# A latent-attention kernel: the next head group's projections one step sooner, and the second query tile's spread sums behind the next group's transposes

## The reference

```
q  = rms_norm(q_lat)  @ w_q_up    # 16 heads of 64 + 32
kv = rms_norm(kv_lat) @ w_kv_up   # 16 heads of 64 + 64
q_nope, q_pe = rms_norm(q[..., :64]), rope(rms_norm(q[..., 64:]))
k_nope, v    = rms_norm(kv[..., :64]), kv[..., 64:]
s = (q_nope . k_nope + q_pe . k_pe) * 96 ** -0.5
p = softmax(s);  o = p @ v;  o = o @ w_out
```

## Time and profile before

| | |
|---|---|
| median of 3 runs | 1421.31 us (1418.82 to 1421.77) |
| the profiled execution | 1419.54 us, of which 1417.7 us is the span of the trace |
| head of group 0 to the end of group 3 in the trace | about 1041.6 to 1195.2 us |
| PE busy (share of the span) | 1327.6 us (94%) |
| DVE, ACT busy | 838.3 us (59%), 553.0 us (39%) |
| instructions | 16585 |

### The profile page before, as it was taken

One profiled execution on the slowest core, in us unless ns is written; L12 is line 12 of the kernel. 1 busy time (PEld: TensorE's weight loads), 2 busy tenths in 40 slices (PEclk: granted clock), 3 DMA queues, 4 the chain that ended last, 5 costly groups with the idle time before them and its releaser, 6 DMA issues.

```text
span 1417.7 us, 16585 instructions
## 1 busy us (share of the span) xinstructions
PE 1327.6 (94%) x6816; PEld 1065.0 (75%) x6816; DVE 838.3 (59%) x1170; ACT 553.0 (39%) x737; POOL 6.5 (0%) x20
## 2 busy tenths in 40 slices
PE   6999879999899999999999999999978878799998
PEld 5877658888777787867777777787866556688887
DVE  5665666668664455662525262527766676667777
ACT  5354354454421222422222222224545555554542
POOL 0000000000000000000000000000000000000000
PEclk9999989999999999999999999999989999899999
DMA  8436375544645532264545444322211130445541
GB/s 325 181 119 252 119 282 186 190 159 180 235 149 208 208 119 90 97 245 163 196 160 190 166 177 180 119 82 70 83 64 36 73 120 13 166 141 205 187 178 60
DMA packets 23926, 218.79 MB, mean 154 GB/s; under 512 B 3120, under 2 KB 8240, under 8 KB 10672
## 3 DMA queue, kind: packets, MB, share of 16 engines
q1 hardware_dynamic: 21472, 209.67, 40.1%
q10 hardware_dynamic: 1520, 4.98, 0.9%
q0 software_dynamic: 864, 3.15, 0.6%
HBM read 216.74 MB, written 1.05 MB: 154 GB/s over the span
## 4 chain that ended last, share of the span: by engine, by line
PE 73%; DVE 14%; ACT 6%; issue 4%; DMA 2%; SPq 0%; DVEq 0%; ACTq 0%
PE bank L503 18%; PE bank L505 17%; PE bank L504 17%; PE bank L515 7%; DVE w_lo L1569 5%; PE bank L516 4%; ACT w_hi L1069 3%; PE mod_ps L552 3%; PE turned L531 2%; PE bank L920 2%; DVE scaled L1610 2%; DVE gated L1924 1%; PE small L928 1%; DMA raw<-in_w_branch 1%; DVE h L1831 1%
## 5 line engine op out<-in xcount | busy, mean ns | idle before, releaser
L1569 DVE TENSOR_TENSOR w_lo<-raw,w_hi 128x2048 fp32r<-128x2048 f32 (+4 forms) x168 | 338.0, 2053 | 84.8 <-ACT w_hi L1069 84.8
L1069 ACT ACTIVATE w_hi<-raw 128x2048 fp32r<-128x2048 f32 (+4 forms) x168 | 280.1, 1715 | 206.5 <-PE bank L505 169.0
L503 PE MATMUL bank<-act_parts,w_hi 128*128 128x512 f32 (+1 forms) x600 | 225.1, 375 | 1.8 <-DVE act_parts L1594 1.8
L515 PE MATMUL bank<-act_parts,w_hi 128*128 128x512 f32 x608 | 216.6, 400 | 6.7 <-DVE act_parts L1594 4.2
L504 PE MATMUL bank<-act_parts,w_hi 128*128 128x512 f32 (+1 forms) x600 | 221.8, 370 | 0.0
L505 PE MATMUL bank<-act_parts,w_lo 128*128 128x512 f32 (+1 forms) x600 | 221.6, 369 | 0.0
L516 PE MATMUL bank<-act_parts,w_lo 128*128 128x256 f32 x608 | 171.4, 282 | 0.0
L503 PE MATMUL bank<-w_hi,h_hi 128*128 128x512 f32 x392 | 155.3, 396 | 7.0 <-DVE h_lo L1846 3.6
L504 PE MATMUL bank<-w_lo,h_hi 128*128 128x512 f32 x392 | 153.4, 391 | 0.0
L505 PE MATMUL bank<-w_hi,h_lo 128*128 128x512 f32 x392 | 153.2, 391 | 0.0
L515 PEld LDWEIGHTS bank<-act_parts,w_hi 128*128 128x128 f32 x608 | 115.5, 190 | 35.1 <-DVE act_parts L1594 4.6
(11 more groups left out here) (262 smaller groups left out, 1650.2 us busy)
## 6 DMA issues: line engine op xcount, KB each, us to landing
raw<-in_ffn SPq DMA_DIRECT2D x35, 2048.0 KB, 7.9
raw<-in_mlp SPq DMA_DIRECT2D x24, 2048.0 KB, 7.8
raw<-in_mod_gate SPq DMA_DIRECT2D x7, 2048.0 KB, 8.0
raw<-in_conv_in SPq DMA_DIRECT2D x8, 1536.0 KB, 7.3
raw<-in_w_gates SPq DMA_DIRECT2D x4, 2048.0 KB, 8.2
raw<-in_w_branch SPq DMA_DIRECT2D x4, 2048.0 KB, 7.9
raw<-in_mla_q SPq DMA_DIRECT2D x4, 1152.0 KB, 5.2
raw<-in_w_out SPq DMA_DIRECT2D x2, 2048.0 KB, 8.3
```

The costliest lines, as they stand in the source:

```text
L503: te.matmul(dst, sh, mh, start=(j == 0), stop=False)
L515: te.matmul(b[:, :].rearrange("p (a t) -> p a t", a=2), sh, act_parts[:, :, 0, j, :], start=(j == 0), stop=False)
L1069: act.activation(w_hi[:, s, part], raw[:, at % 2, part], ACT.Copy).then_inc(hi_ready, 1)
L1569: ve.tensor_tensor(w_lo[:, s, part], raw[:, at % 2, part], w_hi[:, s, part].bitcast(f32), ALU.subtract).then_inc(lo_ready, 1)
```

## The change

Three things are moved; nothing is added or taken away.

1. PE does `project(1)` straight behind `project(0)` in step 0, and each later one a step sooner: steps 0 to 4 hold j = (0, 1), 2, 3, 4, 5, and steps 5 to 7 none.
2. ACT takes (0), (1), (2, 3), (4), (5) in steps 0 to 4, with its squares and its weight split tied to the same `take` as before. DVE's five pieces (`query_sums`, `query_gains`, the split, `query_rotation`, `key_sums`) each go one step up.
3. For groups 0 to 2, `spread_sums` of the second query tile leaves the end of its group and stands in the next group's head, behind the transposes of keys and queries and ahead of the scores.

```diff
--- before.py
+++ after.py
@@ -950,13 +950,16 @@
                 te.wait_ge(qk_ready, n.step("qk"))
                 for t in range(NT):
                     turn([qg[:, t, h, :] for h in range(GH)])
+                if g:
+                    spread_sums(g - 1, 1, mod_ps)
                 te.wait_ge(tr_read, n.at("tr"))
                 for u in range(2):
                     mla_scores(u)
                 trs = []
                 for u in range(8):
-                    if following and u < 6:
-                        project(u)
+                    if following:
+                        for j in ((0, 1), (2,), (3,), (4,), (5,), (), (), ())[u]:
+                            project(j)
                     te.wait_ge(probs_ready, 8 + n.step("probs"))
                     turn([pr[:, u % 2, j * P:(j + 1) * P] for j in range(4)])
                     trs.append(n.at("tr"))
@@ -971,7 +974,8 @@
                         mla_values(g, u // 2 - 1, values_of[u // 6], trs[u - 1])
                     if u == 5:
                         spread_sums(g, 0, sums_of[0])
-                spread_sums(g, 1, sums_of[1])
+                if not following:
+                    spread_sums(g, 1, sums_of[1])
                 mla_values(g, 3, values_of[1], trs[7])
 
             for j in range(NT, 6):
@@ -1472,15 +1476,15 @@
                         o_high(g, g - 1, slice(0, SEQ))
                     if u == 6 and not following:
                         spread_copy(g + 1, 2 * g + 1, mod_ps, slice(0, P))
-                    if following and u < 6:
-                        if u == NT and g:
+                    for j in ((0,), (1,), (2, 3), (4,), (5,), (), (), ())[u] if following else ():
+                        if j == NT and g:
                             act.wait_ge(pv_done, 8 + 4 * g)
-                        take(u, g + 1)
-                        if u == 1:
+                        take(j, g + 1)
+                        if j == 1:
                             squares(True)
-                        if u == 3:
+                        if j == 3:
                             split(width)
-                        if u == 5:
+                        if j == 5:
                             squares(False)
                 if following:
                     group_roots()
@@ -2171,15 +2175,15 @@
                     if u == 4:
                         sums_diag(g, 0)
                     if following:
+                        if u == 1:
+                            query_sums()
                         if u == 2:
-                            query_sums()
+                            query_gains()
                         if u == 3:
-                            query_gains()
+                            split(width)
                         if u == 4:
-                            split(width)
+                            query_rotation()
                         if u == 5:
-                            query_rotation()
-                        if u == 6:
                             key_sums()
                     elif u == 6:
                         o_scaled(g + 1, 4 * g + 2, small, slice(0, P))
```

## The result

The changed kernel took 1413.23 us in the median of 7 runs (1408.10 to 1416.38), the kernel before 1421.31 us of 7 (1417.25 to 1423.31): a ratio of 0.9947, with a 95% interval of 0.9928 to 0.9967. Measured twice more beside other runs of the kernel before, it was 1412.82 against 1419.27 us (0.9959, 0.9944 to 0.9973) and 1413.50 against 1419.23 us (0.9969, 0.9956 to 0.9981). So the gain is 6 to 8 us, where 2.1 were forecast and 1415.6 was the low end of the range.

A forecast was written before the change was run, and what follows sets the result against it. Each group was taken to end when DVE's run without idle time ends. Gains 0.8 + 0.6 + 0.6 by the run and 0.6 by the spread, less 0.5 for the clock, made 2.1 us: 1419.2 from 1421.31, range 1415.6 to 1422.2.

The forecast's parts named there:

- the DVE run: DVE's stretch without idle time up to copy 7, ending each group; 10.84 us before, forecast 10.64, starting with the split.
- The three gains by the run: Groups 0, 1 and 2: copy 7 comes sooner; gains of 0.8, 0.6 and 0.6 us.
- 38 to 38.6: Sign of being right: scores to scores in group 1 takes 38 to 38.6 us in place of 39.00.
- the clock: PE's granted clock at the ends of groups: not expected to be better; 0.5 us taken off the gain.
- A: Rival: PE's clock stays up at one group's end; 5.7 us gained, 1415.6; chance 0.34 including the fuller sum.
- its sign, 1.0 all through a group's end: Granted clock of 1.0 throughout a group's end, named as showing the forecast wrong and A right.
- a full sum: No clock change: sum 2.9 rather than 2.6 us, the 0.5 not lost, 1418.4; shares A's chance of 0.34.
- Its price for one end: In A, up to half of PE's 6.13 us in the low stretch comes back, 3.1 us.
- B: Rival: ACT's work comes 0.6 us later, nothing gained at the run's start; only 0.6 left, 1420.7; chance 0.09.
- C: Rival: low clock holds through next scores and first product, each such group losing 3.0 us; slower; chance 0.07.
- The spread: Second tile's spread moved behind the next head's transposes: 0.3 us gained in groups 0 and 2, 0.6 in all.
- Its cover by ACT's copy of `qgT`: The moved spread's 0.60 us on PE falls within the 0.68 us wait for ACT's `qgT`, costed at nothing.

The follow-up runs named there:

- the two filled ones: Kernel before and changed kernel, each with unread transposes of the identity in PE's waits: 1414.61 us (0.9983) and 1413.47 us (0.9970) against 1418.49.
- e3: Kernel before plus 20 unread transposes of the identity on PE ahead of the second spread, groups 0 to 2: 1414.61 us against 1418.49, ratio 0.9983.
- e2: Changed kernel with the spread put back at the end of its group: 1416.52 us, ratio 0.9990 to the kernel before.
- e5: Changed kernel once more, unaltered: 1412.82 us against 1419.27 for the kernel before, ratio 0.9959.
- e9: Changed kernel again, unaltered, for a third profile: 1413.50 us against 1419.23 for the kernel before, ratio 0.9969.
- e10: Same kernel as e2, measured again: 1414.69 us, ratio 0.9971 to the kernel before.
- e1: Kernel before with only the second tile's spread moved behind the next group's transposes: 1419.88 us against 1418.49, ratio 1.0014.
- e4: Changed kernel plus unread transposes of the identity in PE's waits of steps 6, 7 and group 2's step 5: 1413.47 us against 1418.49, ratio 0.9970.
- the wide filling: e4 plus unread transposes ahead of group 0's query transposes and behind the output projection: 1409.46 and 1409.07 us, ratios 0.9941 and 0.9932 to the kernel before.
- e11: Same kernel as e4, measured again beside the change: 1415.82 us, ratio 0.9977 to the kernel before.
- e7: e4 plus unread transposes ahead of group 0's query transposes and behind the output projection, first measurement: 1409.46 us, ratio 0.9941 to the kernel before.
- e8: e4 with DVE's weight split put back behind the diagonals of step 4: 1418.71 us, ratio 1.0002 to the kernel before.

## Why the prediction was wrong

**What held.** All of the work on the order, nearly to the row. Behind the scores of group 1, transposes 0 were worked out at 8.12 us and stood at 8.10 (1097.46 - 1089.36), transposes 3 at 17.71 and 17.72, the DVE run at 20.06 and 20.01, copy 7 at 30.70 and 30.64. The three gains by the run, 0.8 + 0.6 + 0.6, measured 0.92, 0.65 and 0.71 with the clock up. Group 1 took 36.99 us, less than the 38 to 38.6 named as a sign of being right: 0.65 of the 2.0 us is the run, the rest the clock. In group 2 the order also made a wait that the prediction does not have: the wide split ahead of the diagonals keeps PE waiting 2.16 us before the first spread (1154.53 in the first profile), where the kernel before did not wait.

**The step that failed** is "the clock": "I do not expect the clock to be better, and take 0.5 off". The two unfilled kernels and the two filled ones put numbers to it. Low clock at the ends of groups costs the kernel before 124.79 - 119.20 = 5.6 us, and the change, in the mean of its three profiles, 117.99 - 116.92 = 1.1. The term is 4.5 us gained, not 0.5 lost. Of that, 0.3 is chance: in the first profile the low clock at the front of group 0 ended sooner, so that the first transposes stood 10.10 us behind the scores and not 11.1 to 11.3. At the ends alone the change pays 1.4 us and the term is 4.2. With it: 2.3 + 4.5 = 6.8 us. That this equals 124.79 less 117.99 proves nothing, since the terms are differences of these same profiles; what can be held against it are the medians, 8.1, 6.5 and 5.7.

The reasoning under it had two faults. I took total idle time for what counts ("no less idle time on PE in it, only more pieces"), and an idle stretch of 2.83 us before a drop as a sign that three shorter ones would do the same. The total did stay (2.83 and 0.62 us at the end of group 0 before; 1.32, 0.51 and 1.67 now), but the low stretches went from 17 us to between 10 and 14. And I didn't ask *when* the low stretch would come, which is the larger fault: with PE waiting from step 6 on (step 5 in group 2), a drop comes earlier and is partly over before PE is on the path again. By length alone the price would have gone from 5.6 to between 3.3 and 4.6 us, an estimate in proportion to 10 and 14 of 17; it went to 1.4. What the clock costs at the ends is shown by e3, and that the low stretches lie earlier is read from the profiles; that the earlier idle time is what moves the drop I only infer from e2, e5, e9 and e10, where it is seen.

**The rivals.** A comes nearest, and its sign, 1.0 all through a group's end, was there twice in the first profile; I gave 0.34 to it and to a full sum together. But it says that the clock does not fall, and in e5 and e9 it fell in two groups of three and cost time in one. Its price for one end (3.1 us, by halving PE's busy time in the low stretch) was an upper bound; measured were 1.4 to 2.2 us for each end. B did not occur: ACT's two takes and split came 0.1 us earlier than worked out. C did not occur in any profile of the change.

The Trainium skill, TensorE: Matmul & The Clock Gate (HAM oscillation), puts the harm on long uninterrupted gaps in PE's work. I let the 2.83 us wait speak against it. The runs are on its side only in part: filling the waits kept the clock up at all three ends. But dividing them did not: in e5 the clock fell at the end of group 0 where no wait was longer than 1.33 us.

**The spread.** 0.6 us were expected of its move. It is 0.3 to 0.5 in e1, at low clock, and nothing at 2.4 GHz, since then values to scores take 5.61 us in any order. Its cover by ACT's copy of `qgT` held. What gained in groups 0 and 2 was, by e3, the clock under the spread itself.

**What stays open.** The runs of one kernel scatter by 5 to 11 us, but in the attention the two profiles of the kernel before differ by 0.2 us and the three of the change by 1.2, so most of the scatter is not placed. It goes with the clock: of the 35 runs of the kernel before beside e1 to e4, the seven shortest (1412.5 to 1414.0 us) have a mean granted clock of 0.981 to 0.983, the others 0.974 to 0.980. In which part of the program those seven kept the clock no trace shows, and so it stays open how often the kernel before keeps it at the ends of groups.

## What to carry to other kernels

Where one engine waits at the end of each stage and works alone right after it, read that stage's granted clock before and after: harmless idle time can be paid for in the next few microseconds. Find the stretch in which an engine has no idle time, put its long pieces that are ready early at its front, and move the feeding work with them. When a change redistributes TensorE's waits, price the low clock at every end as a term of its own, from both sides, rather than as a small correction, and look where the low stretch lies now: it may have moved and not gone.

## What the runs showed of the hardware

- Useless work made the kernel faster: 20 transposes (2.35 us) in a wait took 1.4 to 2.2 us off each end of a group; the change and the wide filling together took 10 us off the kernel before. In the changed kernel, filling the ends of groups alone gained nothing in the whole (e4, e11), as the clock then fell at an unfilled wait of group 3.
- What a low stretch costs depends on where it lies: about 7 us of it within group 2 cost nothing in e5 and e9 (40.28 us, as with the clock up), while in the kernel before it cost 2.0 us there.
- With the clock up, PE, DVE and ACT repeat themselves to 0.01 to 0.03 us from profile to profile and from chip to chip (36.98, 36.99, 37.00 us for group 1), so that a sum over rows can be right to 0.1 us, while the time of the whole program scatters by 5 to 11.
- Filling is not free when the clock is already low: 12 transposes took 1.47 us in e7 and 2.75 us in e8, and there overran the wait they were meant to fill.
